# A state-space kernel's shifted rows laid out by DMAs within SBUF instead of by matmuls, in a four-layer model on one core

## The reference

```python
def s5_ssm(u, a_re, a_im, log_dt, b_re, b_im, c_re, c_im, d_skip):
    ...
    bu_re = jnp.einsum('blgp,gnp->blgn', ug, bb_re)
    bu_im = jnp.einsum('blgp,gnp->blgn', ug, bb_im)
    ...
    _, _, x_re, x_im = lax.associative_scan(_complex_affine_combine, (a_seq_re, a_seq_im, bu_re, bu_im), axis=1)
    y = jnp.einsum('blgn,gpn->blgp', x_re, c_re) - jnp.einsum('blgn,gpn->blgp', x_im, c_im)
    y = y + d_skip.astype(f32).reshape(S_GROUPS, S_GROUP) * ug
```

## Time and profile before

| | us |
|---|---|
| median of 3 runs (2448.57 to 2450.28) | 2449.53 |
| the profiled execution, whole time | 2448.28 |
| its span, first to last instruction | 2446.5 |
| TensorE matmuls busy in the span | 2387.8 (98%) |
| VectorE busy | 1469.5 (60%) |
| ScalarE busy | 1080.2 (44%) |
| GpSimd busy | 164.4 (7%) |

### The profile page before, as it was taken

How to read it: one execution, slowest core, us unless ns; L and a number is a source line. 1 busy time by engine, 2 the same in 40 slices (tenths; PEclk the granted TensorE clock), 3 DMA queues, 4 the chain that set the end, 5 groups by cost and what they waited for, 6 DMA issues and landing times.

```text
span 2446.5 us, 33247 instructions
## 1 busy us (share of the span) xinstructions
PE 2387.8 (98%) x11675; PEld 1941.0 (79%) x11675; DVE 1469.5 (60%) x2142; ACT 1080.2 (44%) x1458; POOL 164.4 (7%) x159
## 2 busy tenths in 40 slices
PE   8999999999999999999999999999999989999998
PEld 6767888888788878888887777888888767888887
DVE  7986654532676646455236766887533686687722
ACT  5345433332556644333224644555423473454421
POOL 2011100000100011000002021000011012000000
PEclk9999999999999999999999999999999999999999
DMA  7331233333222222333333102333334202333331
GB/s 175 69 95 52 78 103 94 92 95 100 75 78 77 69 78 86 94 94 99 95 99 93 44 10 86 103 103 94 95 95 125 72 10 61 90 106 94 93 95 64
DMA packets 400952, 209.69 MB, mean 86 GB/s; under 512 B 18131, under 2 KB 397655, under 8 KB 400871
## 3 DMA queue, kind: packets, MB, share of 16 engines
q1 hardware_dynamic: 397111, 199.65, 28.2%
q0 software_dynamic: 3424, 8.91, 1.5%
q10 hardware_dynamic: 336, 0.05, 0.0%
HBM read 204.38 MB, written 4.19 MB: 85 GB/s over the span
## 4 chain that ended last, share of the span: by engine, by line
PE 82%; DVE 12%; ACT 3%; issue 2%; DVEq 1%; DMA 0%; ACTq 0%; SPq 0%
PE bank L677 67%; PE bank L723 4%; DVE tmp L1956 2%; DVE w_lo L1924 2%; PE bank L727 2%; PE bank L1308 1%; DVEq L1953 1%; PE bank L1284 1%; DVE small L2708 1%; PE bank L1259 1%; PE bank L1222 1%; PE bank L1179 0%; ACT w_hi L1382 0%; PE bank L753 0%; PE bank L1118 0%
## 5 line engine op out<-in xcount | busy, mean ns | idle before, releaser
L1924 DVE TENSOR_TENSOR w_lo<-w_raw,w_hi 128x1024 fp32r<-128x1024 f32 x380 | 472.2, 1243 | 540.9 <-ACT w_hi L1382 536.5
L677 PE MATMUL bank<-h_hi,w_hi 128*128 128x512 f32 x1840 | 725.5, 394 | 2.0 <-DVE w_lo L1924 1.0
L677 PE MATMUL bank<-h_lo,w_hi 128*128 128x512 f32 x1840 | 716.8, 390 | 0.0
L677 PE MATMUL bank<-h_hi,w_lo 128*128 128x512 f32 x1840 | 716.1, 389 | 0.0
L1382 ACT ACTIVATE w_hi<-w_raw 128x1024 fp32r<-128x1024 f32 x380 | 402.2, 1059 | 636.7 <-PE bank L677 619.1
L677 PEld LDWEIGHTS bank<-h_hi,w_hi 128*128 128x128 f32 x1840 | 345.6, 188 | 77.0 <-issue 4.0
L677 PEld LDWEIGHTS bank<-h_hi,w_lo 128*128 128x128 f32 x1840 | 345.7, 188 | 72.7 <-issue 2.4
L677 PEld LDWEIGHTS bank<-h_lo,w_hi 128*128 128x128 f32 x1840 | 345.4, 188 | 72.1
L677 PE MATMUL bank<-hid_hi,w_hi 128*128 128x512 f32 x704 | 273.9, 389 | 0.0
L677 PE MATMUL bank<-hid_hi,w_lo 128*128 128x512 f32 x704 | 273.9, 389 | 0.0
L677 PE MATMUL bank<-hid_lo,w_hi 128*128 128x512 f32 x704 | 273.9, 389 | 0.0
(11 more groups left out here) (472 smaller groups left out, 2854.4 us busy)
## 6 DMA issues: line engine op xcount, KB each, us to landing
w_raw<-in_ffn_w SPq DMA_DIRECT2D x120, 512.0 KB, 3.8
w_raw<-in_w_up SPq DMA_DIRECT2D x88, 512.0 KB, 3.7
w_raw<-in_c_w_in SPq DMA_DIRECT2D x32, 512.0 KB, 4.0
w_raw<-in_w_down SPq DMA_DIRECT2D x32, 512.0 KB, 3.6
w_raw<-in_w_in SPq DMA_DIRECT2D x28, 512.0 KB, 3.8
w_raw<-in_w_o SPq DMA_DIRECT2D x16, 512.0 KB, 3.6
w_raw<-in_ab_w_in SPq DMA_DIRECT2D x12, 512.0 KB, 5.8
w_raw<-in_ffn_w SPq DMA_DIRECT2D x16, 384.0 KB, 3.2
```

The costliest lines, as they stand in the source:

```text
L677: mm = nc.tensor.matmul(out[:], w[:, s, k], v[:, kt], start=(kt == 0 and w is w_hi and v is hi), stop=(kt == sum(slabs) - 1 and v is lo))
L1924: nc.vector.tensor_tensor(w_lo[:, s], w_raw[:, s], w_hi[:, s].bitcast(F32), ALU.subtract).then_inc(lo_done, 1)
```

## The change

The taps are stored with the group innermost: `s5_k` is the same 128x512, but ScalarE writes it in the order (w g), and `s5_conv` becomes [128, 8, 16, 32], so that for each `j` a row is one run of 2 KB. GpSimd waits for `s5_k`, issues eight DMAs from `sq_sum` rows 0 to 127 - r to `s5_conv` rows r to 127, and zeroes the rows above with seven memsets. TensorE waits for all of them ahead of `enter`. The eight matmuls and ScalarE's eight copies go. The weights of a group in `leave` are now 128 elements that are 32 elements apart.

```diff
-        s5_conv = m("s5_conv", [P, GROUPS, STEP, GW], 56)
+        s5_conv = m("s5_conv", [P, STEP, GW, GROUPS], 56)
...
-        s5_k = sq_sum[:].rearrange("p (g w) -> p g w", g=GROUPS)
+        s5_k = sq_sum[:].rearrange("p (w g) -> p g w", g=GROUPS)
...
                 pool.dma_start(u_step[GW * k:GW * k + GW], by_step[i]).then_inc(us_loaded, 16)
+            pool.wait_ge(s5_k_ready, 1)
+            for j in range(STEP):
+                r = GW * (STEP - 1 - j)
+                pool.dma_start(s5_conv[r:P, j].rearrange("p w g -> p (w g)"), sq_sum[0:P - r]).then_inc(s5_conv_in, 16)
+            for j in range(STEP - 1):
+                nc.gpsimd.memset(s5_conv[0:GW * (STEP - 1 - j), j], 0.0).then_inc(s5_conv_zero, 1)
             pool.wait_ge(ys_ready, 1)
...
-                pe.wait_ge(prep["scalar_to_pe"], n(prep["scalar_to_pe"]))
-                for j in range(STEP):
-                    out = take(5 + j % 3)
-                    off = P - GW * (STEP - 1 - j)
-                    nc.tensor.matmul(out[:], shifted[:, off:off + P], s5_k.rearrange("p g w -> p (g w)"),
-                                     start=True, stop=True).then_inc(prep["pe_to_scalar"], 1)
...
-                        nc.tensor.matmul(out[:, c:c + CH], s5_conv[:, 8 * i + g].rearrange("p j w -> p (j w)"),
+                        nc.tensor.matmul(out[:, c:c + CH], s5_conv[:].rearrange("p j w g -> p (j w) g")[:, :, 8 * i + g],
                                          u_step[:, 8 * i + g], start=True, stop=False)
...
                 pe.wait_ge(us_loaded, 16 * STEP)
+                pe.wait_ge(s5_conv_in, 16 * STEP)
+                pe.wait_ge(s5_conv_zero, STEP - 1)
                 enter(0)
...
                 nc.scalar.activation(s5_k, bank[4][:].rearrange("p (g w) -> p g w", g=GROUPS), ACT.Copy)\
-                    .then_inc(prep["scalar_to_pe"], 1)
+                    .then_inc(s5_k_ready, 1)
...
-                for j in range(STEP):
-                    act.wait_ge(prep["pe_to_scalar"], n(prep["pe_to_scalar"]))
-                    nc.scalar.activation(s5_conv[:, :, j], bank[5 + j % 3][:].rearrange("p (g w) -> p g w", g=GROUPS),
-                                         ACT.Copy).then_inc(bank_free[5 + j % 3], 1)
```

More of the change, by code:

```diff
@@ L368, in signals @@
                                                      "scalar_to_pe", "vector_to_scalar", "scalar_to_vector")}
-        prep = {k: sem(f"prep_{k}") for k in ("pe_to_scalar", "vector_to_pe", "scalar_to_pe", "vector_to_scalar", "scalar_to_vector")}
+        prep = {k: sem(f"prep_{k}") for k in ("pe_to_scalar", "vector_to_pe", "vector_to_scalar", "scalar_to_vector")}
+        s5_k_ready, s5_conv_in, s5_conv_zero = (sem(k) for k in ("s5_k_ready", "s5_conv_in", "s5_conv_zero"))
         hgrn = signals("hgrn")
```

## The result

| | us |
|---|---|
| after, median of 5 runs (2463.22 to 2464.34) | 2463.79 |
| before, beside it, median of 5 runs (2448.57 to 2450.98) | 2450.00 |
| ratio, 95% interval | 1.0057 (1.0042 to 1.0072) |
| the profiled execution after, whole time | 2463.93 |
| its span | 2462.1 |

The change makes the kernel slower by 0.57% (0.42 to 0.72%). The forecast was 2455.1, +5.6 us, with a range that ended at 2460.0: right in direction, but the measured +13.8 us is more than twice as much.

The account below looks back on a forecast made before the run. VectorE's unbroken run was taken as the bound from 84 to 150 us. Terms 0 + 0 + 0 + 0 + 5.6 us on a 2449.53 median gave 2455.1 us, with an 8-in-10 range of 2447.5 to 2460.

Parts of the forecast that it names:

- Part 5: In leave, 64 strided weight loads each cost 0.111 us more: +7.1 us, +5.6 after 1.47 us of slack.
- Part 4: TensorE idles 5.3 us ahead of enter and loses 1.7 us of clock; hidden by slack, 0 (bad end +3.0).
- The main case: Strided weight loads in leave take twice as long, giving 2455.1 us; chance 0.50.
- What bounds the kernel: From 84 to 150 us VectorE's unbroken run is the bound, with TensorE's work running under it.
- the rival in which this time counts: TensorE time freed before s5_core shows after all, if its bank wait is an artefact: 2442.7 to 2446.3 us; chance 0.05.
- Parts 1 and 2: Removing eight TensorE matmuls (6.86 us) and eight ScalarE copies gains 0; the step-wise s5_k copy takes about 1.0 us.
- Part 3: GpSimd's eight DMAs and seven fills ahead of enter: DMAs landed at 95.5, fills done at 95.0, VectorE not held up.
- Margin 2: Slack at the end of leave: 1.47 us later is free, more goes through one for one to the projections.
- That the load doesn't mind the steps: Rival: strided weight loads in leave cost nothing extra, so 2449.5 us, no change; chance 0.36.
- Fills that hold up VectorE: Rival: GpSimd's fills or DMAs delay VectorE's critical run by up to 7.3 us, 2456.8 us; chance 0.03.
- The new wait as the bound: Rival: late DMAs plus the clock's fall ahead of enter cost up to 3.0 us, 2449.5 to 2452.5; chance 0.06.
- margin 1: Slack at the start of s5_core: it may start 2.8 us later than 97.06 at no cost.

Follow-up runs that it names:

- with everything else mended: Changed kernel with s5_conv in its old layout, DMAs writing 64-byte runs, waits moved ahead of leave, eight idle-data matmuls filling TensorE's hole: 2449.72 us, ratio 1.0004.
- the one before it: Changed kernel with s5_conv in its old layout, DMAs writing 64-byte runs, waits moved ahead of leave, hole not filled: 2450.28 us, ratio 1.0003.
- the front alone: Changed kernel, but leave reads each group's weights as one run of 512 bytes (wrong values): 2452.06 us, ratio 1.0010.
- the stride alone: Kernel before, keeping its eight matmuls and copies, with s5_conv stored group innermost: 2462.21 us, ratio 1.0048.
- the second scan: Kernel before, leave's four quarters reading s5_conv weights 8, 4, 1 and 16 elements apart (wrong values): one run, 2463.32 us.

## Why the prediction was off

Two steps failed. Part 5 reckoned `leave`, and the work behind it, at full clock and had no term for a clock that falls under slow loads; the runs showed 6.9 us for it. Part 4 put the late start of the front at 0, and it cost 2.1 us. The main case itself, the doubled load, was right in mechanism and nearly in size.

*What bounds the kernel* held. VectorE's run hides the eight matmuls: with everything else mended the time was 2449.72, no gain. In that run the front's TensorE time was filled again, but in the one before it, where it was free, no time came of it either (2450.28), and the product started at 108.67, released by VectorE as ever: the rival in which this time counts is refuted.

*Parts 1 and 2* (0 and 0): right. The copy of the taps in steps took 1.16 us, not 1.0.

*Part 3*: right, with some luck in the size. Start of `enter` forecast at 95.5, measured 95.71; but issues took 0.52 us each instead of 0.63 and the last landing 5.9 instead of 5.3, two errors that nearly cancel. The fills took 0.47 instead of 0.6. VectorE's operations beside them took what they took before.

*Part 4* (0) failed in two terms, and the front cost 2.1 us. The first is the clock: I took 1.7 us lost, 3.4 as upper end, from the rows behind a hole of 2.77 us. From the start of `enter` to the product came 97.06 to 107.92 before, 10.86 us, and 95.71 to 111.00 after, 15.29: 4.4 us lost, since half clock lasted until 106 us. The second is the margin. The 2.8 us was how late VectorE could get its data. TensorE's own queue had less: 0.20 us ahead of the product and 0.83 ahead of the last `swap_sums` (the row at 122.70). The product came 2.88 us late, `swap_sums` 3.17, and `leave` 2.08, that is, what was left after some 1.1 us. VectorE was only 0.63 us late (123.44 against 122.81), near the 0.4 by which 3.17 exceeds the margin of 2.8, so for that engine the margin was read about right. I had priced this lateness against the next reader, not against what stands behind it on the same engine. Margin 2, which might have taken up 1.5 of the 2.1 us, was already spent by the load. How long the lower clock lasts is not fixed: in the front alone it lasted until 109.5 us instead of 106.1, `swap_sums` came 4.45 us late, more than the 2.8, and there the lateness did go by way of VectorE.

*Part 5* (+5.6) was right in what it priced. The load went from 0.113 to 0.215 us; the forecast was 0.224, made from VectorE's steps. With the clock kept up it gave +6.0 by the medians (interval 3.9 to 8.3 us) and 5.0 in the trace. The term that is missing is what slower loads do to TensorE's clock: I reckoned `leave` at full clock throughout, 21.5 us. It took 25.60, and the gate products behind it 2.2 more. In the trace the forecast was low by 8.2 us (13.8 against 5.6): 6.9 of the clock and 2.1 of the front, less 0.6 because the load was cheaper than forecast and 0.2 more saved with the hole.

*The rivals.* That the load doesn't mind steps is refuted by every run that reads `s5_conv` 32 elements apart. The Trainium skill had this side in "TensorE: Matmul & The Clock Gate", section "LDWEIGHTS (loading the stationary operand)", by the number of columns alone; the runs disagree, 0.215 against 0.113 us with 128 columns in both. The other side is the Trainium skill's "Advanced Engine Details and Errata", section "SBUF Cachelines", with full speed at two hits on a line of 16 bytes. The runs agree with it: at 2 elements apart there are two hits and the load took 0.12, at 8 and 32 apart one, and it took 0.235 and 0.215. Why 8 is dearer than 32 they don't say. Fills that hold up VectorE: refuted. The new wait as the bound: no, it and the clock behind it are 2.1 of 13.8 us.

*What would show it wrong.* The text said that a product after 109 means that margin 1 is used up; it came at 111.00. It did not ask for the clock in `leave`; with the work behind it, half of the loss was the clock's there. My range added the two uncertain costs but held no case in which TensorE is busy and its clock falls.

What stays open: why the clock came down 6 us into `leave` after the change, 4 us in the run with the stride alone and 3.6 us in the second scan; why the front's lower clock lasted longer in one trace than in another; and distance 4 at full clock.

## What to carry to other kernels

A layout that saves work where an engine has room is paid for where it is read: look at who reads the tensor, how often, and whether that reader's load is what sets its pace. Of an operation that a wait delays, reckon the slack on its own queue first and then that of the engine that reads its result. Where a stretch of TensorE is bound by weight loads under few streamed columns, price every slowdown of the load twice, once at full clock and once with the clock at half, up to the place where dense work follows.

## What the runs showed of the hardware

- **The clock can fall while TensorE shows as busy.** In `leave`, with 64 columns streamed per load: at 0.113 us per load it stayed at 1.00; with half the loads at 0.215 it went to 0.50, and so it did with half of them at 0.12 and then 0.17; with the same loads and 128 or 256 columns streamed per `s5_conv` matmul it stayed at 1.00. Once down, it stayed down through a quarter of plain loads, and came back in the gate products behind `leave`, matmuls of 512 columns.
- **At half clock a strided load costs next to nothing more.** Both kinds took 0.213 us (0.225 at distances 4 and 8). So the price of the stride and that of the clock don't add up in full.
- **The hole behind removed work costs clock wherever it lies.** 5.5 us of idle ahead of `enter`, or 7.05 ahead of the product: in both cases `swap_sums` came at 122.3, 3.2 us late. The same holes in two other runs made it come at 123.59 and at 121.11, so the cost varies by 2.5 us. Six idle matmuls in the hole brought back the front's 2 us.
- **DMAs within SBUF** from GpSimd's queue landed in 1.8 us (32 KB) to 5.9 us (256 KB) in rows of 2 KB. In runs of 64 bytes each issue took 1.08 us instead of 0.52.
- **ScalarE's write in steps of 128 bytes** took 1.16 us for 128x512 instead of 0.60.
- **GpSimd's memset** of up to 112x512 took 0.47 us, as VectorE's.
